# Two attentions rearranged as a pipeline of 128-row tiles

## Chip, core and metric
One core of a Trainium2 chip. The metric is the device time of the whole program in microseconds (us): three runs of the kernel before took 1804.64, 1805.28 and 1810.08 us.

## What is computed
One inference step of a two-layer decoder for 256 prompt tokens and 32 sample tokens (8 sequences of 4 new tokens, each with 256 past positions), all in fp32.

- Layer 0: RMSNorm, q/k/v projection, norm and rotary of each head, attention A with 16 heads of 64, output projection, dense SwiGLU. With 256 positions the block-sparse attention of the reference is a plain causal one. The past keys and values of a sample lie in two pages of 128 positions that a page table names.
- Shared keys and values for layer 1 from the stream behind layer 0.
- Layer 1: q projection for 3 groups x 8 heads, attention B: each head slot attends in three dilated windows and merges the three by their softmax denominators. That is one softmax over the three masked score sets together, with common keys and values. Output projection, then a top-2-of-8 mixture of SwiGLU experts, which takes more than half of the time.

The core of both attentions, from the reference:
```
sc = einsum('qhd,khd->qhk', q, k) * ATTN_SCALE       # masked
p = softmax(sc, axis=-1)                             # B: over its three groups
o = einsum('qhk,khd->qhd', p, v)
```

## The kernel before
Each matmul against weights is three matmuls of fp32r parts (whi, wlo; lines 241 to 243); attention matmuls are plain fp32, and each of those shows as two records. The work is written out by hand in one instruction stream per engine, with semaphores between them: SyncE issues the weight pieces into a ring of six, GpSimd issues the pages of the caches and the stores of new keys and values, TensorE multiplies and transposes, VectorE takes maxima and scales, ScalarE takes exponentials and copies.

Attention (`attend` on TensorE, ScalarE and VectorE) is a loop over ten steps t. Step t handles the prompt scores of head pair t (A) or head t (B), the keys of sample sequence t, the sample scores of t-1, the prompt values of t-1 and the sample values of t-2.

- Prompt scores (`scores`, line 524): per head and group two matmuls, queries 0 to 127 against keys 0 to 127 and queries 128 to 255 against all 256. In A the two heads of a pair lie in the two row halves of the array.
- `masked_max` (line 1202) adds the mask in PSUM and takes the row maximum; `exp` (line 933) writes probabilities with their sums; `probabilities` (lines 1212 to 1218) adds the groups and divides; `turn_probs` (line 567) transposes three blocks; ScalarE copies them (line 916); `values` (line 583) multiplies.
- Keys of a sequence: two page transfers (A: 512 KB each, `paged`, line 361; B: one transfer of both, `window`, line 378). `turn_keys` (line 558) transposes four 128x128 blocks at a time; ScalarE and in A VectorE copy them (lines 909, 1190).
- Sample scores of one sequence (line 541): for each pair of heads one matmul with a block-diagonal query block (`query_block`) of 64 columns in A and 96 in B, 288 key columns, all added up in one bank.
- Sample values of one sequence: transposes (line 593), then 16 matmuls in A and 8 in B with 128x128 value weights and 8 columns of probabilities (line 602). The new tokens' values of all sequences are one matmul for each pair at the very end (line 631).
- Output is split into high and low parts (lines 972 and 1296), then the output projection starts.

GpSimd's order (`caches`): keys of q, then values of q-1; keys wait for TensorE's transposes of the sequence that held the buffer, values for sample values three sequences back. The stores of new keys and values (lines 342, 343) stand behind the keys of sequence 0.

## Time and profile before

| | |
|---|---|
| median of three runs | 1805.28 us |
| profiled execution | 1809.19 us |
| its span | 1807.5 us |
| TensorE busy | 1710.8 us (95%) |
| VectorE busy | 1365.8 us (76%) |
| ScalarE busy | 1038.7 us (57%) |
| GpSimd busy | 56.0 us (3%) |
| mean granted TensorE clock | 0.958 |

The rows come from one execution, taken by the hardware profiler. PE is TensorE's matmuls, PEld its weight loads (beside them), DVE VectorE, ACT ScalarE, POOL GpSimd, SP SyncE. L12 is line 12 of the kernel. A granted clock of 1.00 is 2.4 GHz, 0.50 is 1.2 GHz. The page cuts the span in 40 slices of 45.2 us; attention A lies in slices 3 to 6, attention B in slices 14 to 16, the experts from slice 18 on. Ends of matmuls are modelled, and the busy time of matmuls that overlap is counted once. "<-" behind an idle time names what ended it. A chain of waits is followed back from the last instruction and shows what each stretch of time hung on.

### The profile page before, as it was taken

The page shows a single profiled execution, that of the slowest core. Times are in us where ns is not written, and L with a number is a line of the kernel's source. Part 1 is how long each engine was busy: PE and PEld are TensorE (multiplying, and loading weights), DVE is VectorE, ACT ScalarE, POOL GpSimd, SP SyncE. Part 2 cuts the span into 40 slices and gives each one's busy share as a digit, 9 for nine tenths or more (in the row PEclk, how much of TensorE's full clock was granted, in tenths as well). Part 3 has the DMA queues.
Part 4 walks back from the last instruction along what each step waited for, and adds up shares of the span by engine and source line. Part 5 has one row for each costly group of instructions (what it writes and reads, how often), then busy time and mean ns, then how long its engine had stood idle before and what let it go on. Part 6 is the DMA issues. An engine that isn't in the chain of part 4 may idle for free.

```text
span 1807.5 us, 24840 instructions
## 1 busy us (share of the span) xinstructions
PE 1710.8 (95%) x9068; PEld 1431.7 (79%) x9068; DVE 1365.8 (76%) x1732; ACT 1038.7 (57%) x1043; POOL 56.0 (3%) x81
## 2 busy tenths in 40 slices
PE   7998989999989798589999999999999999999998
PEld 6876779999987677467887888888878878878886
DVE  5864426565567685688898898898898888888987
ACT  5433324433444242457777777777777767777775
POOL 0001101000000110100000000000000000000000
PEclk9999869999999887699999999999999999999999
DMA  9346413543653421169999999999999999999995
GB/s 326 111 155 189 141 37 126 165 149 114 191 171 117 154 98 44 47 233 330 354 350 331 364 340 343 352 347 331 364 335 344 353 338 351 347 337 354 351 334 205
DMA packets 232982, 452.97 MB, mean 251 GB/s; under 512 B 7585, under 2 KB 79265, under 8 KB 232785
## 3 DMA queue, kind: packets, MB, share of 16 engines
q1 hardware_dynamic: 224656, 421.93, 66.8%
q0 software_dynamic: 8256, 30.12, 5.1%
q8 instruction: 43, 0.70, 0.2%
q14 instruction: 27, 0.21, 0.0%
HBM read 447.30 MB, written 4.72 MB: 250 GB/s over the span
## 4 chain that ended last, share of the span: by engine, by line
PE 86%; DVE 8%; ACT 3%; issue 2%; DMA 1%; POOLq 0%; DVEq 0%; SPq 0%; ACTq 0%; POOL 0%
PE psum L241 24%; PE psum L243 23%; PE psum L242 23%; PE psum L602 2%; PE psum L541 2%; PE psum L740 1%; PE psum L775 1%; PE psum L558 1%; PE psum L755 1%; DVE wlo L237 1%; ACT whi L233 1%; DVE rs L1152 1%; PE psum L583 1%; PE psum L479 1%; PE psum L488 1%
## 5 line engine op out<-in xcount | busy, mean ns | idle before, releaser
L237 DVE TENSOR_TENSOR wlo<-raw,whi 128x2048 fp32r<-128x2048 f32 (+1 forms) x404 | 911.7, 2262 | 208.1 <-ACT whi L233 207.7
L233 ACT ACTIVATE whi<-raw 128x2048 fp32r<-128x2048 f32 (+1 forms) x404 | 764.9, 1896 | 304.4 <-PE psum L243 304.3
L241 PE MATMUL psum<-whi,xgh 128*128 128x512 f32 x896 | 359.7, 401 | 8.5 <-DVE wlo L237 7.1
L243 PE MATMUL psum<-whi,xgl 128*128 128x512 f32 x896 | 355.7, 397 | 0.0
L242 PE MATMUL psum<-wlo,xgh 128*128 128x512 f32 x896 | 354.5, 396 | 0.0
L241 PE MATMUL psum<-hh,whi 128*128 128x288 f32 x800 | 248.4, 310 | 13.7 <-DVE hl L1296 9.1
L243 PE MATMUL psum<-hh,wlo 128*128 128x288 f32 x800 | 241.8, 302 | 0.0
L242 PE MATMUL psum<-hl,whi 128*128 128x288 f32 x800 | 241.1, 301 | 0.0
L241 PEld LDWEIGHTS psum<-whi,xgh 128*128 128x128 f32 x896 | 169.1, 189 | 50.6 <-DVE wlo L237 10.6
L243 PEld LDWEIGHTS psum<-whi,xgl 128*128 128x128 f32 x896 | 168.8, 188 | 41.1
L242 PEld LDWEIGHTS psum<-wlo,xgh 128*128 128x128 f32 x896 | 169.2, 189 | 39.1
L241 PE MATMUL psum<-whi,acth 128*128 128x512 f32 x448 | 178.3, 398 | 0.0
L242 PE MATMUL psum<-wlo,acth 128*128 128x512 f32 x448 | 178.2, 398 | 0.0
L243 PE MATMUL psum<-whi,actl 128*128 128x512 f32 x448 | 175.9, 393 | 0.0
L241 PEld LDWEIGHTS psum<-hh,whi 128*128 128x128 f32 x800 | 155.0, 194 | 22.1 <-DVE hl L1296 9.5
L242 PEld LDWEIGHTS psum<-hl,whi 128*128 128x128 f32 x800 | 155.3, 194 | 1.3
L243 PEld LDWEIGHTS psum<-hh,wlo 128*128 128x128 f32 x800 | 154.5, 193 | 0.0
L241 PEld LDWEIGHTS psum<-whi,acth 128*128 128x128 f32 x448 | 84.1, 188 | 20.7
L243 PEld LDWEIGHTS psum<-whi,actl 128*128 128x128 f32 x448 | 84.1, 188 | 20.5
L242 PEld LDWEIGHTS psum<-wlo,acth 128*128 128x128 f32 x448 | 84.2, 188 | 18.7
L1063 ACT ACTIVATE sg<-psum 128x512 f32<-128x512 f32 x56 | 33.5, 598 | 47.8 <-PE psum L243 47.7
L241 PE MATMUL psum<-gh,whi 128*128 128x288 f32 x176 | 52.1, 296 | 1.2 <-issue 1.2
(297 smaller groups left out, 1751.8 us busy)
## 6 DMA issues: line engine op xcount, KB each, us to landing
raw<-in_w_gu_moe SPq DMA_DIRECT2D x226, 1024.0 KB, 5.2
raw<-in_w_down_moe SPq DMA_DIRECT2D x112, 1024.0 KB, 5.3
raw<-in_w_gu_dense SPq DMA_DIRECT2D x22, 1024.0 KB, 5.1
raw<-in_w_qkv_a SPq DMA_DIRECT2D x12, 1024.0 KB, 12.8
raw<-in_w_down_dense SPq DMA_DIRECT2D x16, 704.0 KB, 4.6
kraw_a<-in_cache_a_k POOLq DMA_DIRECT2D x16, 512.0 KB, 4.6
vraw_a<-in_cache_a_v POOLq DMA_DIRECT2D x16, 512.0 KB, 4.8
raw<-in_w_q_b SPq DMA_DIRECT2D x6, 1024.0 KB, 5.0
```

The lines of the kernel that those rows point to most:

```text
L233: nc.scalar.activation(whi[:, p % SPL, 0:size], raw[:, p % RAW, 0:size], ACT.Copy).then_inc(hi_ready, 1)
L237: nc.vector.tensor_tensor(wlo[:, p % SPL, 0:size], raw[:, p % RAW, 0:size], whi[:, p % SPL, 0:size].bitcast(F32), ALU.subtract).then_inc(p ...
L241: nc.tensor.matmul(out, lh, rh, start=start, stop=False)
L242: nc.tensor.matmul(out, lh, rl, start=False, stop=False)
L243: return nc.tensor.matmul(out, ll, rh, start=False, stop=stop)
L479: nc.tensor.matmul(ps[6][:, 0:T], con("rot"), sq[:, 5 + r % 2], start=True, stop=True)\
L488: nc.tensor.matmul(bank[:, 0:T], cst[c:c + 32, slice(*CONST["headspread"])], rs[c:c + 32, 1], start=True, stop=True)\
L541: ins = nc.tensor.matmul(ps[SS_BANK][0:rows, 0:T], b["qblk"][:, u % 2, j * rows:(j + 1) * rows], b["keys"][:, j, :], start=j == 0, stop=j ...
L558: ins = nc.tensor.transpose(bank[:, i * P:(i + 1) * P], b["kraw"][:, u % b["nk"], pg, j * P:(j + 1) * P], con("ident"))
L583: ins = nc.tensor.matmul(out, b["vtok"][:, half, h * DH:(h + 1) * DH], b["pt"][:, h % 2, cols_], start=half == 0, stop=half == 1)
L602: ins = nc.tensor.matmul(out, b["vraw"][:, u % 2, c, j * P:(j + 1) * P], b["spt"][:, u % 2, c, 8 * j:8 * j + 8], start=c == 0, stop=c == 1)
L1063: nc.scalar.activation(sg[:, :], ps[0][:, :], ACT.Silu).then_inc(sem("silu_done"), 1)
```

## The change
Both attentions become a loop over jobs (`JOBS_A`, `JOBS_B`). A job is one 128-row tile of softmax: a prompt head ("p"), or a sample tile ("s"). A sample tile holds four pairs of heads x four sequences x two heads x four queries = 128 rows: four tiles in A, two in B.

In step t TensorE does the scores of job t, transposes the probabilities of job t-2 and multiplies the prompt values of job t-2; sample values of a tile come in steps t-3 and t-4 counted the same way. `FILLS` says how many key pages (now 128 positions x 512 columns, 256 KB) are transposed in each step: in A two in each of 16 steps, in B 4, 4, 0, 3, 3, 2.

Sample scores of a tile: for each group and each of four sequences four matmuls with 32 query columns, one to each 32-column group of the array, 288 key columns. Sample values: probabilities are the 32-column weights and the values stream, 128 columns at a time; the new tokens' values are one matmul of 512 columns for each column group. ScalarE scales the result by the denominators (`scale_out`), and `pick_rows` brings it back to head layout with eight matmuls.

The key buffer has six places in A and four in B, the value buffer four and three. A has three score banks in rotation; B has one set of three. GpSimd issues single key pages, and values of half a width in A, in an order given by `VALUES_A` and `VALUES_B`: the list holds for each value transfer the number of the key page behind which it is issued. In B the query block lies where the tokens of the new keys lay, so it waits for their stores. The masks of the samples grow in B; a constant of 32 columns goes.

```diff
+P_, S_ = "p", "s"
+JOBS_A = [(P_, 0), (P_, 1), (P_, 2), (P_, 3), (S_, 0), (P_, 4), (P_, 5), (P_, 6), (S_, 1), (P_, 7), (P_, 8), (P_, 9), (S_, 2),
+          (P_, 10), (P_, 11), (P_, 12), (S_, 3), (P_, 13), (P_, 14), (P_, 15)]
+JOBS_B = [(P_, 0), (P_, 1), (S_, 0), (P_, 2), (P_, 3), (P_, 4), (S_, 1), (P_, 5), (P_, 6), (P_, 7)]
+FILLS_A = [2] * 16
+FILLS_B = [4, 4, 0, 3, 3, 2]
+VALUES_A = [9] * 4 + [16, 16, 18, 18] + [24, 24, 26, 26] + [32] * 4
+VALUES_B = [7] * 3 + [16] * 5
...
+        A["score_banks"], A["pt_bank"], A["pv_bank"], A["kt_banks"], A["s_bank"] = ((0,), (1,), (7,)), 2, 3, (4, 5), 6
...
+        B["score_banks"], B["pt_bank"], B["pv_bank"], B["kt_banks"], B["s_bank"] = ((0, 1, 2),), 3, 4, (5, 7), 6
...
+            def key_page(b, n):
+                tg, slot = b["tag"], n % b["kring"]
+                z, q, page = n // 8, 4 * (n // (2 * b["nj"])) + n // 2 % 4, n % 2
+                if n >= b["kring"]:
+                    eng.wait_ge(sem(f"ktr_done_{tg}"), n - b["kring"] + 1)
+                if b is A:
+                    pg = eng.value_load(pgt[0:1, 2 * q + page:2 * q + page + 1], min_val=0, max_val=NPHYS - 1)
+                    src = io["cache_a_k"][0][bass.ds(pg, 1), :, 512 * (z % 2):512 * (z % 2) + 512].rearrange("a p n -> p (a n)")
+                else:
+                    src = io["cache_b_k"][q][P * page:P * page + P, :]
+                eng.dma_start(b["kraw"][:, slot, :], src).then_inc(sem(f"kraw_loaded_{tg}{slot}"), 16)
...
+            def value_pages(b, n):
+                tg, slot = b["tag"], n % b["vring"]
+                z, q = n // 4, 4 * (n // b["nj"]) + n % 4
+                if n >= b["vring"]:
+                    eng.wait_ge(sem(f"spv_done_{tg}"), n - b["vring"] + 1)
+                if b is A:
+                    for j in range(2):
+                        pg = eng.value_load(pgt[0:1, 2 * q + j:2 * q + j + 1], min_val=0, max_val=NPHYS - 1)
+                        eng.dma_start(b["vraw"][:, slot, j, :], io["cache_a_v"][0][bass.ds(pg, 1), :, 512 * (z % 2):512 * (z % 2) + 512]
+                                      .rearrange("a p n -> p (a n)")).then_inc(sem(f"vraw_loaded_{tg}{slot}"), 16)
+                else:
+                    eng.dma_start(b["vraw"][:, slot], io["cache_b_v"][q].rearrange("(j p) n -> p j n", p=P)).then_inc(sem(f"vraw_loaded_{tg}{slot}"), 32)
...
+            def caches(b, first):
+                v = 0
+                for n in range(first, 4 * b["nj"]):
+                    key_page(b, n)
+                    if n == first + 3:
+                        eng.wait_ge(sem(f"kv_stored_{b['tag']}"), 64)
+                    while v < 2 * b["nj"] and b["vafter"][v] == n:
+                        value_pages(b, v)
+                        v += 1
+                while v < 2 * b["nj"]:
+                    value_pages(b, v)
+                    v += 1
+            for n in range(A["kring"]):
+                key_page(A, n)
...
+            caches(A, A["kring"])
...
+                def banks_free(k):
+                    if k >= len(b["score_banks"]):
+                        eng.wait_ge(sem(f"exped_{tg}"), exped_count(b, k - len(b["score_banks"])))
...
+                def scores(k, h):
+                    banks_free(k)
+                    r, j = 64 * (h % 2), h // 2
+                    for g in range(ng):
+                        bank = ps[job_banks(b, k)[g]]
+                        q = b["qT"][r:r + 64, g * nj + j, :]
+                        nc.tensor.matmul(bank[:, 0:P], q[:, 0:P], b["kT"][r:r + 64, j, 0:P], start=True, stop=True)
+                        nc.tensor.matmul(bank[:, P:384], q[:, P:2 * P], b["kT"][r:r + 64, j, 0:2 * P], start=True, stop=True)                            .then_inc(sem(f"scored_{tg}"), 1)
...
+                def sample_scores(k, z):
+                    banks_free(k)
+                    eng.wait_ge(sem(f"keys_copied0_{tg}"), 4 * (z + 1))
+                    eng.wait_ge(sem(f"keys_copied1_{tg}"), 4 * (z + 1))
+                    eng.wait_ge(sem(f"new_keys_{tg}"), z + 1)
+                    eng.wait_ge(sem(f"qblk_{tg}"), z // (nj // 4) + 1)
+                    for g in range(ng):
+                        for s in range(4):
+                            for c in range(4):
+                                at_ = (4 * g + s) * b["qrow"] + 32 * (4 * z % nj + c)
+                                ins = nc.tensor.matmul(ps[job_banks(b, k)[g]][32 * c:32 * c + 32, 0:T], b["qblk"][:, at_:at_ + 32],
+                                                       b["keys"][:, s, c, :], start=s == 0, stop=s == 3)
+                        ins.then_inc(sem(f"scored_{tg}"), 1)
+                def turn_keys(n):
+                    slot = n % b["kring"]
+                    eng.wait_ge(sem(f"kraw_loaded_{tg}{slot}"), 16 * (n // b["kring"] + 1))
+                    if n >= 2:
+                        eng.wait_ge(sem(f"keys_copied{n % 2}_{tg}"), n // 2)
+                    for c in range(4):
+                        ins = nc.tensor.transpose(ps[b["kt_banks"][n % 2]][:, c * P:(c + 1) * P], b["kraw"][:, slot, c * P:(c + 1) * P], con("ident"))
...
+                def turn_probs(k, kind):
+                    eng.wait_ge(sem(f"probs_{tg}"), k + 1)
+                    if k >= 1:
+                        eng.wait_ge(sem(f"pt_copied_{tg}"), k)
+                    bank, p = ps[b["pt_bank"]], b["p"][:, k % b["ps"], 0]
+                    for c in range(2):
+                        nc.tensor.transpose(bank[:, c * P:(c + 1) * P], p[:, c * P:(c + 1) * P], con("ident"))
+                    w = P if kind == P_ else NSAMP
+                    nc.tensor.transpose(bank[0:w, 2 * P:3 * P], p[:, 2 * P:2 * P + w], con("ident")).then_inc(sem(f"pt_turned_{tg}"), 1)
...
+                def values(k, h):
+                    eng.wait_ge(sem(f"pt_copied_{tg}"), k + 1)
+                    if h % 2 == 0 and h >= 2:
+                        eng.wait_ge(sem(f"o_copied_{tg}"), h // 2)
+                    out, v = ps[b["pv_bank"]][64 * (h % 2):64 * (h % 2) + 64], b["vtok"][:, :, h * DH:(h + 1) * DH]
+                    nc.tensor.matmul(out[:, 0:2 * P], v[:, 0], b["pt"][:, h % 2, 0:2 * P], start=True, stop=False)
+                    nc.tensor.matmul(out[:, P:2 * P], v[:, 1], b["pt"][:, h % 2, 2 * P:3 * P], start=False, stop=True)                        .then_inc(sem(f"pv_done_{tg}"), 1)
...
+                def sample_values(k, z, part):
+                    j0 = 4 * z % nj
+                    if part == 0:
+                        eng.wait_ge(sem(f"pt_copied_{tg}"), k + 1)
+                        if z >= 1:
+                            eng.wait_ge(sem(f"so_copied_{tg}"), z)
+                        for c in range(4):
+                            new = b["vtok"][0:NSAMP, 2, (j0 + c) * P:(j0 + c + 1) * P].unsqueeze(1).to_broadcast([NSAMP, 4, P])
+                            nc.tensor.matmul(out_bank[32 * c:32 * c + 32, :].rearrange("p (s n) -> p s n", s=4),
+                                             b["spt"][0:NSAMP, 2 * P + 32 * c:2 * P + 32 * c + 32], new, start=True, stop=False)
+                    for s in (0, 1) if part == 0 else (2, 3):
+                        n = 4 * z + s
+                        slot = n % b["vring"]
+                        eng.wait_ge(sem(f"vraw_loaded_{tg}{slot}"), 32 * (n // b["vring"] + 1))
+                        for half in range(2):
+                            for c in range(4):
+                                ins = nc.tensor.matmul(out_bank[32 * c:32 * c + 32, s * P:(s + 1) * P],
+                                                       b["spt"][:, half * P + 32 * c:half * P + 32 * c + 32],
+                                                       b["vraw"][:, slot, half, c * P:(c + 1) * P], start=False, stop=s == 3 and half == 1)
+                        ins.then_inc(sem(f"spv_done_{tg}"), 1)
...
+                def pick_rows(z):
+                    eng.wait_ge(sem(f"so_scaled_{tg}"), z + 1)
+                    for s in range(4):
+                        for r in range(2):
+                            ins = nc.tensor.matmul(out_bank[64 * r:64 * r + 64, 16 * s:16 * s + 16], b["pvs"][:, s * P + 64 * r:s * P + 64 * r + 64],
+                                                   pick[:, s, r], start=True, stop=True)
+                    ins.then_inc(sem(f"picked_{tg}"), 1)
...
+                for t in range(len(b["jobs"]) + 3):
+                    kind, u = job_at(b, t)
+                    fills = fills_at(b, t)
+                    if kind == P_:
+                        scores(t, u)
+                    elif kind == S_:
+                        sample_scores(t, u)
+                    for n in fills[0:1]:
+                        turn_keys(n)
+                    kind2, u2 = job_at(b, t - 2)
+                    if kind2:
+                        turn_probs(t - 2, kind2)
+                    kind3, z = job_at(b, t - 3)
+                    if kind3 == S_:
+                        sample_values(t - 3, z, 0)
+                    kind4, z = job_at(b, t - 4)
+                    if kind4 == S_:
+                        sample_values(t - 4, z, 1)
+                    for n in fills[1:]:
+                        turn_keys(n)
+                    kind5, z = job_at(b, t - 5)
+                    if kind5 == S_:
+                        pick_rows(z)
+                    if kind2 == P_:
+                        values(t - 2, u2)
...
+                def scale_out(z):
+                    eng.wait_ge(sem(f"spv_done_{tg}"), 4 * (z + 1))
+                    nc.scalar.activation(b["pvs"][:, :], ps[b["s_bank"]][:, :], ACT.Copy, scale=b["sst"][:, z % 2, 8:9])                        .then_inc(sem(f"so_scaled_{tg}"), 1)
...
+                for t in range(len(b["jobs"]) + 3):
+                    fills = [n for n in fills_at(b, t) if n % 2 == 0]
+                    for n in fills[0:1]:
+                        copy_keys(n)
+                    kind2, u2 = job_at(b, t - 2)
+                    if kind2:
+                        copy_probs(t - 2, kind2, u2)
+                    kind5, z = job_at(b, t - 5)
+                    if kind5 == S_:
+                        scale_out(z)
+                    for n in fills[1:]:
+                        copy_keys(n)
+                    kind, u = job_at(b, t)
+                    if kind:
+                        exp(t, kind, u)
+                    kind3, h = job_at(b, t - 2)
+                    if kind3 == P_ and h % 2 == 1:
+                        eng.wait_ge(sem(f"pv_done_{tg}"), h + 1)
+                        nc.scalar.activation(b["oT"][:, h // 2, 0:SEQ], ps[b["pv_bank"]][:, 0:SEQ], ACT.Copy).then_inc(sem(f"o_copied_{tg}"), 1)
...
+                def new_keys(z):
+                    if z >= 1:
+                        eng.wait_ge(sem(f"scored_{tg}"), scored_count(b, b["jobs"].index((S_, z - 1))))
+                    for i in range(4):
+                        ins = V.tensor_copy(b["keys"][:, i, :, PAST:T], b["kT"][:, 4 * z % nj:4 * z % nj + 4, SEQ:T])
+                    ins.then_inc(sem(f"new_keys_{tg}"), 1)
...
+                def query_block(gr):
+                    if gr == 0:
+                        if ng > 1:
+                            eng.wait_ge(sem(f"kv_stored_{tg}"), 64)
+                        chain(V.memset(b["qblk"][:, :], 0.0))
+                    else:
+                        eng.wait_ge(sem(f"scored_{tg}"), scored_count(b, b["jobs"].index((S_, groups - 1))))
...
+                for t in range(len(b["jobs"]) + 3):
+                    kind, u = job_at(b, t)
+                    if t == (0 if ng == 1 else 1):
+                        query_block(0)
+                        new_keys(0)
+                    kind1, u1 = job_at(b, t - 1)
+                    if kind == P_:
+                        masked_max(t, u)
+                    elif kind == S_:
+                        sample_max(t, u)
+                    for n in fills_at(b, t):
+                        if n % 2 == 1:
+                            copy_keys(n)
+                    if kind1 == P_:
+                        probabilities(t - 1, u1)
+                    elif kind1 == S_:
+                        sample_probs(t - 1, u1)
+                        if u1 + 1 < 2 * groups:
+                            new_keys(u1 + 1)
+                        if u1 == groups - 1:
+                            query_block(1)
+                    kind5, z = job_at(b, t - 5)
```

## Rows read from the trace of the kernel before

**Rows 1.** The page's row of the granted clock in tenths, 40 slices.
```profile
PEclk9999869999999887699999999999999999999999
```

**Rows 2.** Chain of waits, attention A: start us, us, what ran.
```profile
127.66 1.03 DVE qblk_a L1169
...
160.42 0.80 PE psum L583 x8
...
165.09 0.86 PE psum L524 x8
165.95 1.02 PE psum L558 x8
...
167.78 0.48 PE psum L567 x3
...
169.46 3.55 PE psum L602 x32
...
265.87 0.61 PE psum L241
```

**Rows 3.** Grouped lines of attention A: count, busy us, mean ns, idle before.
```profile
L541 PE MATMUL psum<-keys_a,qblk_a 128*64 128x288 f32 x128 | 40.4, 479 | 1.0 <-DVE keys_a L1190 1.0
L602 PE MATMUL psum<-spt_a,vraw_a 128*128 128x8 f32 x256 | 34.2, 274 | 0.5 <-ACT sptn_a L952 0.5
...
L1190 DVE COPY keys_a<-psum 128x512 f32<-128x512 f32 x16 | 11.1, 691 | 9.0 <-PE psum L558 9.0
```

**Rows 4.** Windows in attention A: length, busy of PE, PEld, DVE, ACT, POOL, PEclk, DMA, GB/s.
```profile
136.00:140.00 4.00, 2.20 (x14) 1.04 (x12) 2.17 (x11) 0.59 (x2) 1.59 (x3) 1.00 0.92 248
140.00:144.00 4.00, 2.60 (x15) 2.60 (x16) 1.09 (x3) 1.08 (x2) 0.00 (x0) 0.75 0.78 288
190.00:195.00 5.00, 5.00 (x16) 2.29 (x14) 0.00 (x0) 0.00 (x0) 0.48 (x1) 0.68 0.65 213
```

**Rows 5.** Timeline of GpSimd: start us, us, engine, line, what, idle before.
```profile
134.29 0.55 POOL L361 DMA_DIRECT2D kraw_a<-in_cache_a_k  x1 [3.74 <-issue]
136.39 0.53 POOL L361 DMA_DIRECT2D kraw_a<-in_cache_a_k  x1 [1.54 <-issue]
...
147.52 0.53 POOL L361 DMA_DIRECT2D kraw_a<-in_cache_a_k  x1 [0.61 <-issue]
149.01 0.53 POOL L361 DMA_DIRECT2D vraw_a<-in_cache_a_v  x1 [0.97 <-issue]
150.15 0.53 POOL L361 DMA_DIRECT2D vraw_a<-in_cache_a_v  x1 [0.61 <-issue]
...
618.14 0.52 POOL L343 DMA_DIRECT2D out_bv<-vtok_b  x1
```

**Rows 6.** Timeline of TensorE in the q/k/v projection.
```profile
56.08 0.69 PE L471 MATMUL psum<-sq,cst 128*32 128x288 f32 x8
56.70 0.75 PE L479 MATMUL psum<-sq,cst 128*128 128x288 f32 x2
```

**Rows 7.** Chain of waits, attention B.
```profile
615.43 4.72 DMA kraw_b<-in_cache_b_k
...
648.34 2.16 PE psum L524 x12
...
663.40 0.79 PE psum L583 x4
...
713.03 0.61 PE psum L241
```

**Rows 8.** Timeline of all engines in one step of attention B.
```profile
644.22 0.17 DVE L1212 RECIPROCAL st_b<-st_b 128x2 f32<-128x2 f32 x1
...
645.80 0.35 DVE L1218 TENSOR_SCALAR p_b<-p_b,st_b 128x256 f32<-128x256 f32 x1
...
650.53 0.30 DVE L1202 CUSTOM_DVE_ANT_0 psum<-psum,mask_b 128x128 f32<-128x128 f32 x1 [0.26 <-PE psum L524]
...
654.41 0.21 ACT L933 ACTIVATION_READ_ACCUMULATOR p_b<-psum,st_b 128x1 f32 x1
```

More of the change, by code:

```diff
@@ new lines, in job_banks, with job_at, exped_count, scored_count @@
+        def job_banks(b, k):
+            return b["score_banks"][k % len(b["score_banks"])]
+        def job_at(b, k):
+            return b["jobs"][k] if 0 <= k < len(b["jobs"]) else ("", 0)
+        def exped_count(b, k):
+            return sum(2 if kind == P_ else 1 for kind, _ in b["jobs"][:k + 1])
+        def scored_count(b, k):
+            return b["ng"] * (k + 1)
+        def fills_at(b, t):
+            n = sum(b["fills"][:t])
+            return range(n, n + b["fills"][t]) if t < len(b["fills"]) else range(0)
@@ L696, in _ @@
             to_tokens(B)
[L697 removed]
+            attend(B)
             residual(P_WOB, tiles_wob, B["nj"], "wob", "o_split_b", hh, hl)
@@ L1611, in prompt, with sample @@
         return np.concatenate([m[0:P, 0:P], m[P:, :]], axis=1)
[L1613 to L1620 removed]
+    def sample(ok, gr):
+        pos = PAST + (i % QLEN)[:, None]
+        new = np.arange(NSAMP)[None, :]
+        own = new // QLEN == 4 * gr + (i[:, None] // 8) % 4
+        return ok(pos, np.arange(PAST)[None, :]), own & ok(pos, PAST + new % QLEN)
     causal = lambda q, k: k <= q
```

457 lines of the change are left out of this document (121 added, 336 removed).

## The prediction

> **What bounds the kernel now.** I read the page first: TensorE is busy 95% of the span, but its granted clock dips in slices 5 and 6 and in slices 14 to 17 of 45.2 us each, and those are the two attentions and what follows them [rows 1]. The expert stage behind them is dense and at full clock, and the change does not touch it, so only the length of the two attention stages can move. Then the chain of waits for attention A. It runs from 127.6 us (first scores) to 265.9 us (first matmul of the output projection), 138.3 us, and from 155 us on it is almost only TensorE: per sequence the sample scores, the prompt scores, page transposes, probability transposes, sample values and prompt values, one behind the other [rows 2]. The grouped lines say which are dear: sample scores (L541) 40.4 us, sample values (L602) 34.2 us [rows 3]. Both are wasteful. L541 streams 288 columns for 64 useful output columns; L602 loads 128x128 weights to stream 8 columns (32 records in 3.55 us, 0.11 us each). The stage windows show a second loss: between 190 and 195 us the clock is 0.68 with TensorE always busy, just behind such an L602 burst, and it falls to 0.75 after 136 to 140 us, where TensorE waited for pages [rows 4]. Attention B runs from about 615.0 to 713.0 us, 98 us [rows 7], and its timeline shows VectorE and ScalarE on the path too: maxima and exponentials of one tile take 4.09 us (650.53 to 654.62) [rows 8].
>
> **The change, attention A.** The new stage has 20 jobs (16 prompt heads, 4 sample tiles of 128 rows). TensorE's work, at full clock:
> - Prompt scores: two matmuls a head, 384 columns. Twelve records for three such pairs take 2.16 us [rows 7], so 0.72 us; 16 x 0.72 = 11.5 us. (Before, two heads in two row halves took 0.86 us [rows 2]; that overlap is lost, 4.6 us dearer in all.)
> - Prompt values: one head alone took 0.79 us [rows 7], two heads in two column halves 0.80 us [rows 2], so this overlap is lost too: 16 x 0.8 = 12.8 us.
> - Probability transposes: 20 x 0.48 = 9.6 us; key pages: 32 times four transposes, eight take 1.02 us, so 16.3 us [rows 2].
> - Sample scores: 64 matmuls as before, but each fills a 32-column group and four neighbours go to four groups. The trace has exactly this form: the head sums, four 128x32 matmuls (8 records) over 288 columns of different data; the next matmul starts 0.62 us later, while one 128x128 matmul of the same width shows 0.75 us [rows 6]. So four go in the time of one: 16 waves x 0.62 = 9.9 us against 40.4.
> - Sample values: per tile 32 matmuls over 128 columns in 8 waves, and four over 512 columns with 32 rows. No row has this. From below: 128/288 of 0.62 = 0.28 us a wave; from above: 8 records alone at L602's 0.11, 0.88 us. I take 0.35, nearer to the form of rows 6; the wide wave is 512/288 x 0.62 = 1.1 us. A tile 3.9 us, four 15.6 (between 13 and 33).
> - Picking rows: eight small matmuls a tile; from 0.6 us (half of L602's rate) to 1.8 us. I take 1.2, in all 4.8.
>
> Sum 80.5 us. Waits come on top. Prompt values stand one page behind the transposes whose ScalarE copy they need; after fills end nothing is between. I take 0.5 us (0 to 0.9) for each of 20 jobs, 10 us. VectorE's work on a tile of A is at most half of that on a tile of B (maxima 2.1 and probabilities 1.9 us [rows 8], one group in place of three), 20 x 2 us, plus 16 page copies at 0.69 us [rows 3], some 51 us; ScalarE has a similar share: neither binds. The chain of one tile spans three steps and is hidden.
>
> What can hurt is GpSimd's queue. It issues, in order, 26 key pages (six stand loaded) and 32 value halves of 256 KB, where it issued 30 transfers of 512 KB; each needs a page number read first. Neighbouring issues are 1.14 us apart (149.01, 150.15), 1.49 when the kind changes (147.52, 149.01), once 2.10 (134.29, 136.39) [rows 5]. I take 1.3: 58 x 1.3 = 75 us, from about 131 us to 206. It is as long as TensorE's own 80, and the two wait for each other: behind key page 9 stand eight value issues, 10 us with no key page, while TensorE needs two pages a job. Value pages wait for sample values of earlier tiles, and keys queue behind them. Landing adds 4.7 us [rows 7]. I charge 6 us for this coupling and, since TensorE stands for some us in that burst, 3 us of half clock. Last, splitting the output stays (265.9 minus the end of the last copy, 4.8 us). End: 127.6 + 80.5 + 10 + 6 + 3 + 4.8 = 231.9, say 230 since the last values overlap. Against 265.9: 36 us saved (10 to 53).
>
> The Trainium skill (DMA: Bandwidth & Descriptors, Anatomy of one DMA) gives about 2 us plus the bytes at 436 GB/s, an estimate of 2.6 us for 256 KB; the trace shows 4.7 us for 512 KB, longer than the 3.2 of that rule. By it pages would land 2 us earlier and the sum would stay, since issue and not landing sets the pace here.
>
> The skill (TensorEngine Tiling (Array Packing), Key Properties) says that a change of tiling mode drains the array, which speaks against more, smaller jobs. By the trace such changes lie inside the durations I use (0.86 to 1.02 us pieces that follow one another directly [rows 2]); some 25 further changes at 0.1 us would be an estimate of 2.5 us.
>
> **Attention B.** Here one set of three score banks serves all jobs, so a job's scores wait for the exponentials of the one before. A prompt step: scores 2.16 us, with the maxima of the first two groups beside them; of the 4.09 us for maxima (2.1) and exponentials two thirds of the maxima (1.4) are hidden; 2.16 + 2.7 + 0.1 = 4.9 us. VectorE must fit the probabilities of the tile before (644.22 to 646.15, 1.9 us [rows 8]) and page copies into that gap of 2.7 us: I add 0.5, 5.4 us (4.9 to 6.5). A sample step: 12 waves x 0.62 = 7.4, then 2.3 for last maximum and a wider exponential: 9.7. Everything else of TensorE hides in the gaps. The start is slow: pages 4 to 7 stand behind the four store issues, which end at 618.7 now with one page issue before them [rows 5] and near 620.2 with four shorter ones; the pages land at 625 to 626; the query block is now written where the keys of the stores lie, so VectorE waits for those stores to land (about 625) with the maxima of job 1 queued behind, then writes block and new keys (4 us), maxima and page copies (3.5 us): the first sample job starts near 632.5. Then 2 x 9.7 + 6 x 5.4 = 51.8, to 684.3; the last tile's probabilities, transposes, copy, values, copy and splitting 7.1 us: 691.4. Half clock in the waits of the start 1.5: 693 against 713.0, 20 us saved (5 to 31).
>
> **The start.** Six key pages (1.5 MB) are fetched where 1 MB was, in the weight-bound first 45 us: the 0.5 MB more cost up to 1.4 us; I take 1. The constants lose 32 columns and the B mask grows, both away from any wait: nothing.
>
> **Sum.** 1 - 36 - 20 = -55 us. The profiled execution of before took 1809.2 us (span 1807.5, 1.7 around it), so its counterpart would be 1754; the median of the runs is 1805.3, and from it 1750 us.
>
> **Rivals.**
> - No waits: tiles flow and GpSimd keeps ahead at 1.14 us (66 us, done at 197). For it: TensorE and the queue need the same time. Against: in-order coupling. A ends at 127.6 + 80.5 + 4.8 = 213 (-53), B at its lower bound (-29): 1805 + 1 - 82 = 1724.
> - GpSimd's queue paces A at 2.1 us an issue, as once in rows 5: 58 x 2.1 = 122 us, last issue at 253, then landing, last sample tile and splitting, 271: A +5, B -20, start +1: 1791. Against: the other intervals are 1.14 and 1.49.
> - Column groups do not run together: 64 sample-score matmuls at 0.5 us, 32 us (+22), values 41 us (+25), A at 277 (+11); in B 96 score matmuls 48 us against 15 on the chain (+33), 713 + 13: 1805 + 25 = 1830. It decides from about half of the overlap lost. Against: rows 6, whose records overlap.
> - Half clock through both stages: a TensorE that works in pieces between waits is granted 1.2 GHz. Each us of TensorE's work costs one more: A +80 less what the queue hides (15), B +27: 55 saved against 92 lost, 1842; slower from some 60% of the work at half clock. For it: after the wait of 136 to 140 us the clock fell to 0.75 [rows 4]. Against: the same window shows 1.00 at 55% busy; only a longer stand or an L602 burst was followed by a fall, and those bursts vanish. The Trainium skill (TensorE: Matmul & The Clock Gate, Part 1) has the clock set by how busy TensorE was shortly before; the rows agree as far as they go.
>
> **How the numbers follow.** Forecast 0.63, no waits 0.18, slow queue 0.10 (0.02 of it no change), groups serial 0.05, half clock 0.04 (0.01 of it no change). Predicted 1750. Range: from the no-waits case, 1722, to the slow queue, 1790; it takes in A 10 to 53 and B 5 to 31 but not all ends at once. A change within 0.3% (5 us) can't be told from none here. Faster 0.89, same 0.03, slower 0.08.
>
> **What would show it.** Attention A's projection starts near 230 us, B's stage is about 78 us long. The sample-score line costs 10 us in A and 15 in B; sample values 16 us in A. GpSimd issues A's pages 1.1 to 1.5 us apart almost without idling between 135 and 206 us, and TensorE's largest wait in A is for key pages. In B scores wait for ScalarE's exponentials each job. The expert stage keeps its length. I am wrong if head groups show up one after another, if the clock row stays at 5 through either stage, or if the saving sits in another stage.

## The result and the profile after

The changed kernel takes 1783.03 us (median of 4 runs, 1781.34 to 1783.73) against 1807.68 for the kernel before on the same chip (4 runs): ratio 0.9865, 95% interval 0.985 to 0.988. It is 25 us faster, where 55 were forecast. All other ratios below are also against the kernel before, measured beside the experiment.

First the page: span 1782.0 us (before 1807.5), and its clock row, to be laid beside [rows 1].

```profile
span 1782.0 us, 25119 instructions
PEclk9997789999999777699999999999999999999999
kraw_a<-in_cache_a_k POOLq DMA_DIRECT2D x32, 256.0 KB, 3.3
```

The dips are still there: 7 and 7 in slices 4 and 5 (134 to 223 us), and slices 14 to 17. The third line says that a key page of 256 KB lands 3.3 us after its issue.

I measure each stage from its first prompt scores to the first matmul of the output projection, and count how many us of it ran at 1.2 GHz (a granted clock of 0.5) and not at 2.4. The windows' mean clock agrees: A's 0.77 is 1 less half of 54.4 in 120.3. (The expectations below carry these counts about 2 us too high, 56.5 for A and 52 for B.) From one profiled execution of each:

| | before | after | forecast |
|---|---|---|---|
| A, length | 138.2 (127.6 to 265.9) | 120.3 (127.8 to 248.1) | 102.4 |
| A, at 1.2 GHz | 48.8 | 54.4 | a cost of 3 |
| A, TensorE waits for key pages | 4.0 | 16.3 | a cost of 6 |
| B, length | 98.0 (615.0 to 713.0) | 93.4 (594.1 to 687.5) | 78 |
| B, at 1.2 GHz | 31.7 | 50.1 | a cost of 1.5 |
| between A and B | 349.1 | 346.0 | 349 |
| after B | 1094.5 | 1094.5 | same |

So 17.9 us came from A, 4.6 from B, 3.1 from the stretch between (5.6 us less of it at 1.2 GHz). The start, for which 1 us more was forecast, took 0.2 more. The windows of both stages, A and B of the kernel before, then A and B of the changed one, columns as in [rows 4]:

```profile
127.62:265.87 138.25, 123.53 (x753) 93.98 (x753) 51.38 (x198) 45.00 (x139) 18.59 (x34) 0.82 0.41 132
614.98:713.03 98.05, 85.58 (x464) 65.33 (x464) 70.26 (x373) 34.15 (x94) 14.06 (x20) 0.84 0.29 98
```
```profile
127.80:248.08 120.28, 94.96 (x797) 61.44 (x797) 45.24 (x183) 44.04 (x123) 33.72 (x62) 0.77 0.47 147
594.10:687.55 93.45, 75.17 (x590) 49.27 (x590) 49.81 (x196) 28.10 (x62) 16.93 (x28) 0.73 0.31 104
```

TensorE is busy 95 of 120 us in A, and the mean granted clock of the stage is 0.77. The grouped lines of A answer to [rows 3] (columns: count, busy us, mean ns, idle before):

```profile
L593 PE MATMUL psum<-cst,kraw_a 128*128 128x128 f32 x128 | 26.2, 342 | 16.7 <-DMA kraw_a<-in_cache_a_k 16.3 <-DVE keys_a L1234 0.4
L634 PE MATMUL psum<-vraw_a,spt_a 128*32 128x128 f32 x256 | 9.6, 296 | 0.0
L582 PE MATMUL psum<-keys_a,qblk_a 128*32 128x288 f32 x128 | 8.6, 408 | 0.4
L646 PE MATMUL psum<-cst,pvs_a 128*64 128x16 f32 x64 | 3.4, 241 | 2.3 <-ACT pvs_a L981 2.3
```

The sample scores (L582) went from 40.4 to 8.6 us and the sample values (L634, with 5.1 us at L626) from 34.2 to 14.7, to which the picks (L646) add 3.4: the part of the change that looked most daring worked. What grew is in the first line: 16.3 us in which TensorE stood for a key page. GpSimd's timeline (columns as in [rows 5]) shows where they come from:

```profile
155.52 0.54 POOL L395 DMA_DIRECT2D kraw_a<-in_cache_a_k  x1 [0.62 <-issue]
163.07 0.54 POOL L407 DMA_DIRECT2D vraw_a<-in_cache_a_v  x1 [7.02 <-PE psum L634]
...
173.72 0.54 POOL L407 DMA_DIRECT2D vraw_a<-in_cache_a_v  x1 [0.60 <-issue]
174.87 0.54 POOL L395 DMA_DIRECT2D kraw_a<-in_cache_a_k  x1 [0.61 <-issue]
...
190.90 0.54 POOL L407 DMA_DIRECT2D vraw_a<-in_cache_a_v  x1 [9.75 <-PE psum L634]
...
218.44 0.54 POOL L407 DMA_DIRECT2D vraw_a<-in_cache_a_v  x1 [10.62 <-PE psum L634]
```

GpSimd mostly issues 1.14 to 1.16 us apart, and stands three times, 7.0, 9.8 and 10.6 us, for the sample values that free a place for a value page. Behind the first two of these stands wait key pages whose places have long been free (that of page 17 since 154.5 us, that of page 25 since 179.4); behind the third wait value pages alone. So TensorE's 16.3 us have three sources: 10.2 us for key pages 17, 19, 25 and 27, behind the first two stands; 3.7 us for page 10, behind eight value issues (139.5 to 147.4 us) that wait for nothing; and 2.4 us for page 6, which lands 7.4 us after its issue, beside the four stores. Pages are counted from 0. The chain of waits shows the other end of the queue, and what the clock does next:

```profile
130.30 7.98 DMA out_av<-vtok_a
...
148.58 3.30 DMA kraw_a<-in_cache_a_k
...
156.93 0.59 PE psum L593 x4
...
163.80 2.15 PE psum L582 x32
...
174.87 3.35 DMA kraw_a<-in_cache_a_k
178.26 1.12 PE psum L593 x4
...
202.65 3.30 DMA kraw_a<-in_cache_a_k
205.99 1.12 PE psum L593 x4
...
248.08 0.61 PE psum L279
```

Key page 19, for instance, is issued at 174.87, lands at 178.2, and TensorE waits for it. Behind it the same four transposes take 1.12 us instead of 0.59: TensorE has stood, and the granted clock is at 0.5 from 169.8 to 186.9. It is so again from 200.5 to 214.2, behind the stand that ends at 199.0 and through that before 206.0, and from 149.3 to 156.1, which begins in the stand for page 10.

B, from its chain of waits, to be laid beside [rows 7]:

```profile
595.61 4.71 DMA kraw_b<-in_cache_b_k
...
614.28 6.03 PE psum L582 x96
...
639.24 1.04 PE psum L593 x4
640.92 1.86 PE psum L626 x8
642.78 1.86 PE psum L634 x32
644.64 1.05 PE psum L593 x4
645.69 1.05 PE psum L614 x2
647.16 6.20 PE psum L582 x96
...
653.84 1.01 PE psum L634 x32
...
675.87 4.04 DMA vraw_b<-in_cache_b_v
...
687.55 0.61 PE psum L279
```

96 sample scores take 6.03 us (7.4 forecast). But the prompt step from 636.2 to 647.2 takes 11.0 us where 5.4 were forecast. Nearly all of it is TensorE's work, and from 637.4 on, at 1.2 GHz, its pieces have twice their length: the same 32 sample values take 1.86 us at 642.78 and 1.01 at 653.84.

### The profile page after: what moved, and what is told of

Its sections match the earlier page's. It is cut to its first block, busy times and chain, and to the rows that moved or that the text cites. A ratio compares the mean times of both kernels' runs of the same rounds, so it can differ in the third digit from the quotient of the medians.

```text
span 1782.0 us, 25119 instructions
## 1 busy us (share of the span) xinstructions
PE 1669.5 (94%) x9238; PEld 1382.0 (78%) x9238; DVE 1339.1 (75%) x1540; ACT 1032.0 (58%) x995; POOL 76.3 (4%) x121
## 4 chain that ended last, share of the span: by engine, by line
PE 85%; DVE 6%; ACT 3%; issue 2%; DMA 2%; POOLq 0%; POOL 0%; DVEq 0%; SPq 0%; ACTq 0%
PE psum L279 24%; PE psum L281 23%; PE psum L280 23%; PE psum L783 1%; PE psum L818 1%; PE psum L593 1%; DVE wlo L275 1%; PE psum L798 1%; PE psum L569 1%; PE psum L582 1%; ACT whi L271 1%; DVE rs L1187 1%; PE psum L568 1%; PE psum L523 1%; PE psum L634 1%
## 5 line engine op out<-in xcount | busy, mean ns | idle before, releaser
L279 PEld LDWEIGHTS psum<-whi,xgh 128*128 128x128 f32 x896 | 169.4, 189 | 50.9 <-DVE wlo L275 10.6
L279 PEld LDWEIGHTS psum<-hh,whi 128*128 128x128 f32 x800 | 153.5, 192 | 21.3 <-DVE hl L1320 9.0
L1098 ACT ACTIVATE sg<-psum 128x512 f32<-128x512 f32 x56 | 33.6, 600 | 47.8 <-PE psum L281 47.7
```

The costliest lines, as they stand in the source:

```text
L279: nc.tensor.matmul(out, lh, rh, start=start, stop=False)
L1098: nc.scalar.activation(sg[:, :], ps[0][:, :], ACT.Silu).then_inc(sem("silu_done"), 1)
```

## The experiments

**Is it the order of issues in A?** The only edit is behind which key page each value page is issued.

```
-VALUES_A = [9] * 4 + [16, 16, 18, 18] + [24, 24, 26, 26] + [32] * 4
+VALUES_A = [10, 11, 12, 13] + [19, 19, 21, 21] + [27, 27, 29, 29] + [32] * 4
```

> Against the changed kernel (1783.0 us median, attention A 120.3 us from first scores to projection, 56.5 us of it at half clock, 16.3 us of TensorE waiting for key pages). Only the order of GpSimd's transfers in A is changed: first four values spread behind key pages 10 to 13, the next ones behind 19 and 21, 27 and 29. Theory O (three times key pages stand behind value issues that wait for sample values; TensorE stands, and half clock follows): the waits for key pages fall from 16 us to under 5, half clock in A to under 35 us, A takes 95 to 103 us, the kernel 1759 to 1767 us. Rival C (TensorE's other short gaps keep the clock low whatever the pages do): the page waits go, but half clock stays near 50 us, A takes 106 to 112 us, 1769 to 1775 us. Rival Q (GpSimd's issue rate of 1.14 us is the limit itself): under 4 us change, 1779 to 1784 us.

Measured: 1762.45 us, ratio 0.9757 (0.9738 to 0.9777), 20.6 us below the changed kernel. A's window:

```profile
127.70:233.91 106.21, 88.69 (x796) 55.85 (x797) 45.14 (x183) 43.47 (x123) 33.64 (x62) 0.84 0.53 167
```

A is 106.2 us, 33.6 at 1.2 GHz, page waits 6.7. The kernel's time and the clock are where theory O had them; A and the page waits are a little over its bounds, in a profiled execution that was the slowest of five (1769.9 us). The number of issues and their pace (1.15 us) did not change, so a queue that is slow in itself (rival "slow queue") is ruled out as what lengthened A.

A second order goes further, one value page at a time between keys:

```
+VALUES_A = [11, 12, 14, 15] + [19, 20, 21, 22] + [27, 28, 29, 30] + [32] * 4
```

> As the first reordering (which gave 1762.5 us and A of 106.2 us, still 6.7 us of waits for key pages), but with single value transfers spread between single key pages: behind 11, 12, 14, 15, then 19 to 22, then 27 to 30. Theory O: waits for key pages 2 to 5 us, A 100 to 105 us, the kernel 1756 to 1762 us. Rival: the 1.14 us an issue is the bound by now (58 issues, 66 us, and stores ahead): 1761 to 1765 us.

Measured: 1760.84 us, ratio 0.974 (0.972 to 0.9759). A is 99.1 us. Its window and its waits (waiter, waited for: us in total, times, longest):

```profile
127.80:226.92 99.12, 84.09 (x796) 53.98 (x796) 45.22 (x183) 43.66 (x123) 33.62 (x62) 0.88 0.57 179
```
```profile
POOL vraw_a L407 <- PE psum L634: 6.9, 3, 5.0
PE psum L593 <- DMA kraw_a<-in_cache_a_k: 4.1, 2, 2.5
```

And the same two of the changed kernel:

```profile
POOL vraw_a L407 <- PE psum L634: 28.6, 4, 10.6
PE psum L593 <- DMA kraw_a<-in_cache_a_k: 16.3, 6, 3.7
```

GpSimd's stands fall from 28.6 to 6.9 us, TensorE's from 16.3 to 4.1 (2.5 of it for page 6, as before), its busy time from 95.0 to 84.1 with the same work: 21 us of A by order alone. By the kernel's time the two orders can't be told apart (0.974 and 0.9757, intervals overlapping).

**What all of A's supply costs.** The 26 key pages past the first six are not fetched in A; the tiles are computed from what the ring holds. The value pages are fetched and waited for as before.

```
+                if b is A and n >= b["kring"]:
+                    return
...
-                    eng.wait_ge(sem(f"kraw_loaded_{tg}{slot}"), 16 * (n // b["kring"] + 1))
+                    eng.wait_ge(sem(f"kraw_loaded_{tg}{slot}"), 16 if b is A else 16 * (n // b["kring"] + 1))
```

> Attention A without the 26 later key pages: they are not fetched, the transposes read the six pages loaded at the start again (this part of the computation is left out); values are fetched as before, with the same waits. It is the lower end of what page supply can cost. Theory O: TensorE never stands for keys, A takes 92 to 100 us, the kernel 1755 to 1763 us, half clock under 30 us. Rival C: A 104 to 112 us, half clock over 45 us, 1767 to 1775 us. If values are what TensorE waits for, A stays above 112 us.

Measured: 1753.31 us, ratio 0.9717 (0.9693 to 0.9741). A's window:

```profile
127.60:218.56 90.96, 79.66 (x797) 50.92 (x797) 45.13 (x183) 43.50 (x123) 19.70 (x36) 0.92 0.37 120
```

A is 91.0 us, a little under theory O's 92 to 100, so 29.3 of its 120.3 us hang on key pages. TensorE's busy time falls from 95.0 to 79.7 us for the same number of matmuls, which is 15.3 of the 29.3; the other 14.0 are idle time (the 16.3 of page stands are gone, waits elsewhere grew by 2.3). For the 15.3 the clock is the candidate (54.4 us at 1.2 GHz in the changed kernel, 13.7 here), which the next run tests. The order of e7 brings back 21 of the 29.

**The clock's part alone.** The order of the transfers stays; 128 idle transposes of constants stand in front of five waits for key pages.

```
-                    eng.wait_ge(sem(f"kraw_loaded_{tg}{slot}"), 16 * (n // b["kring"] + 1))
...
+                    if b is A:
+                        for _ in range({10: 20, 17: 30, 19: 24, 25: 30, 27: 24}.get(n, 0)):
+                            nc.tensor.transpose(ps[b["kt_banks"][n % 2]][:, 0:P], con("featsum"), con("ident"))
+                    eng.wait_ge(sem(f"kraw_loaded_{tg}{slot}"), 16 * (n // b["kring"] + 1))
```

> The changed kernel, GpSimd's order as it is, with 128 idle 128x128 transposes on TensorE in A: 20 to 30 just ahead of each of its waits for key pages 10, 17, 19, 25 and 27 (0.11 us each at full clock). Theory O with clock: the stand for pages stays as idle or filled time (16 us), but TensorE is not slow behind it: half clock in A falls from 56 us to 25 to 40, A from 120 to 108 to 115 us, the kernel 1771 to 1778. Rival (half clock in A costs nothing, since the pages set the time): A 119 to 124 us, 1782 to 1787.

Measured: 1774.63 us (1768.78 to 1780.48), ratio 0.9824 (0.9801 to 0.9847). A's window:

```profile
126.50:234.54 108.04, 91.50 (x924) 63.98 (x924) 44.86 (x183) 43.67 (x123) 33.61 (x62) 0.96 0.52 164
```

A is 108.0 us, with 8.1 at 1.2 GHz: 12.3 us shorter with GpSimd's order unchanged, so the clock had a cost of its own. This profiled execution was the fastest of the four; by the medians the kernel is 8.4 us faster. The transposes themselves take some 14 us (127 of them recorded, at 0.11 us), of which the waits hide only a part, so the clock's cost in A is larger than what this run gives back. The Trainium skill (TensorE: Matmul & The Clock Gate, Part 1) has the clock follow how busy TensorE was shortly before. The trace agrees: transposes without any use raised A's mean granted clock from 0.77 to 0.96.

**Do the column groups run together?** The two inner loops of the sample scores change places, so that four neighbours go to one column group.

```
-                        for s in range(4):
-                            for c in range(4):
+                        for c in range(4):
+                            for s in range(4):
```

> The changed kernel with the two inner loops of the sample scores exchanged: the four sequences of one 32-column group follow one another, so neighbouring matmuls use the same group. Same number of matmuls and same sums. In the changed kernel 32 records take 2.15 us in A and 96 take 6.1 us in B. If column groups run together only when neighbours use different groups: the four tiles of A take 6.5 to 8 us each (+18 to +23 us in all), the two of B 19 to 24 us each (+26 to +36), the kernel 1815 to 1840 us (A may hide some behind pages). If the overlap does not depend on order (records pipelined anyway): within 3 us of 1783.

Measured: 1803.87 us, ratio 0.9978 (0.9968 to 0.9988). The chain of waits of this kernel, one tile of A and one of B:

```profile
161.36 5.10 PE psum L582 x32
...
616.88 13.13 PE psum L582 x96
```

The same 32 records take 5.10 us against 2.15, 96 take 13.1 against 6.03. B is 109.9 us (+16.5), A 124.4 (+4.1). So the groups do run together in the changed kernel, and nearly all of its gain over the kernel before (20.8 of 24.7 us) hangs on the order of two loops. The loss was smaller than I expected (tiles of 6.5 to 8 us in A, the kernel at 1815 or more): it is a factor of 2.2 to 2.4, not of 4. Four neighbours in one group also add up in the same place of PSUM; whether the group or that place holds them apart, no run tells.

**B: a late value page?** The ring gets a fourth place, in the places of two key pages that are no longer needed.

```
-            kraw=70656, ktok=78848, qblk=78848, spt=85120, mask=86656, kring=4, vring=3, ps=2, jobs=JOBS_B, fills=FILLS_B))
+            kraw=70656, ktok=78848, qblk=78848, spt=85120, mask=86656, kring=4, vring=4, ps=2, jobs=JOBS_B, fills=FILLS_B))
...
+                if b is B and n == 3:
+                    eng.wait_ge(sem(f"ktr_done_{tg}"), 14)
```

> In attention B the value buffer gets a fourth place, over the key places of pages 12 and 13 once these are transposed, so that all four sequences of a sample tile are loaded before the first is used; before, the last value page was issued at 675.9 us, when a place came free, and TensorE stood 4.0 us for it. Theory: B is 93.6 us long, becomes 87 to 91, the kernel 1777 to 1780 us. Rival: the sample part is beside the last tile's own chain (exponentials, probabilities, transposes, copy) and nothing is saved, 1782 to 1784 us.

Measured: 1782.27 us, ratio 0.9871 (0.9843 to 0.9899): no difference from the changed kernel. TensorE no longer waits for a value page, B is 95.2 us, 55.5 at 1.2 GHz, where 87 to 91 were expected: the rival holds. The chain's piece "675.87 4.04 DMA" is the transfer's own time; TensorE's own stand for value pages in B was 0.8 us, and taking it away gained nothing.

**B: the clock?** 60 idle transposes in the places where TensorE stands for VectorE and ScalarE.

```
+                WARM = {} if b is A else {0: 16, 1: 8, 3: 4, 4: 4, 5: 4, 8: 8, 9: 8, 10: 8}
...
+                    if t and t in WARM:
+                        if t >= 3:
+                            eng.wait_ge(sem(f"pt_copied_{tg}"), t - 2)
+                        warm(WARM[t])
...
+                    if t == 0:
+                        warm(WARM.get(0, 0))
```

> Attention B with idle transposes of 128x128 on TensorE where it waits anyway: 16 behind the first scores, 8 ahead of the scores of jobs 1, 8, 9 and 10, four ahead of those of jobs 3, 4 and 5; in all 60, 13 us of work at full clock. They wait for nothing and give nothing. Theory W (the low clock in B comes from the gaps that TensorE waits in, and it is what makes B's steps long): half clock in B falls from 52 us to under 35, B takes 84 to 90 us against 93.6, the kernel 1773 to 1780 us. Rival (B hangs on VectorE's and ScalarE's chain, clock is beside): B 94 to 100 us since the added work is partly in the way, 1783 to 1790 us.

Measured: 1778.89 us, ratio 0.9844 (0.9821 to 0.9868). B's window:

```profile
597.50:686.04 88.54, 72.74 (x651) 48.61 (x651) 48.66 (x196) 28.29 (x62) 16.87 (x28) 0.87 0.33 109
```

B is 88.5 us with 22.3 at 1.2 GHz (50.1 in the changed kernel). The 13 us that I gave for the transposes were wrong: 60 at 0.11 us are 6.6. The clock rose, but the gain in time is not settled by this run. The two intervals against the kernel before overlap, and B's length, 4.9 us shorter here, was anything from 90.8 to 93.7 us in five profiled executions with unchanged code in B (the changed kernel, e1, e4, e6, e7).

**B: supply and clock together.** First the 12 later key pages and the 5 later value pages of B are not fetched; then the same with 86 idle transposes (the expectation says 90).

```
+                if b is B and n >= b["kring"]:
+                    return
...
+                if b is B and n >= b["vring"]:
+                    return
...
-                    eng.wait_ge(sem(f"kraw_loaded_{tg}{slot}"), 16 * (n // b["kring"] + 1))
+                    eng.wait_ge(sem(f"kraw_loaded_{tg}{slot}"), 16 if b is B else 16 * (n // b["kring"] + 1))
...
-                        eng.wait_ge(sem(f"vraw_loaded_{tg}{slot}"), 32 * (n // b["vring"] + 1))
+                        eng.wait_ge(sem(f"vraw_loaded_{tg}{slot}"), 32 if b is B else 32 * (n // b["vring"] + 1))
```
```
+                WARM = {} if b is A else {0: 16, 1: 12, 3: 6, 4: 8, 5: 8, 6: 4, 8: 8, 9: 10, 10: 8, 11: 6}
```

> Attention B without the supply of pages: the 12 later key pages and the 5 later value pages of B are not fetched (the tiles are computed from what the ring holds). The forecast had B at 78 us, the changed kernel takes 93.4. Theory (half clock and TensorE's own pieces at that clock): only the stand for a value page near 676 us goes (at most 3 us), B is 88 to 93 us, with 45 us or more at 1.2 GHz. Rival (B waits for its supply as A did): B falls by 8 us or more, to 85 or less, and the half clock falls with it below 30 us.

> The same kernel without the later pages of B, and 90 idle transposes (0.11 us each at full clock, 9.9 us) in the places where TensorE stands for VectorE and ScalarE in B. Theory (half clock is what lengthened B's steps): half clock falls below 20 us and B to 80 to 86 us; what is then left above 78 is the last two jobs, whose sample values, picks and copies follow one another. Rival (the steps are set by the exponentials' chain and by VectorE whatever the clock): B stays at 88 us or more with the clock up.

Measured: without pages 1783.33 us, ratio 0.9863 (0.9843 to 0.9882); with the transposes too 1772.03 us, ratio 0.9799 (0.9782 to 0.9816). B's windows, first without pages, then with transposes:

```profile
596.70:686.22 89.52, 71.09 (x590) 46.96 (x591) 49.60 (x196) 28.20 (x62) 6.82 (x11) 0.78 0.13 44
```
```profile
591.10:675.00 83.90, 72.54 (x676) 50.69 (x677) 48.75 (x196) 28.17 (x62) 6.79 (x11) 0.90 0.13 46
```

Without pages B is 89.5 us, within the theory's bounds of 88 to 93, with 39.1 at 1.2 GHz (45 or more were expected), and the run as a whole gained nothing. With the transposes, B is 83.9 us with 16.5 at 1.2 GHz. The times of the two runs do not overlap (1781.6 to 1785.0 and 1770.8 to 1772.8), so here the transposes' gain is clear of noise. The theory holds for B: its supply hardly matters, its clock does. Not all of the 11.3 us between the two medians need be B's (5.6 in the profiles); A, whose code is the same in both, was 120.9 and 117.4 us in the two profiled executions.

**Order and transposes together.** The order of e7, the transposes of e5 in B, and 20 more in A's last steps.

```
+VALUES_A = [11, 12, 14, 15] + [19, 20, 21, 22] + [27, 28, 29, 30] + [32] * 4
+                WARM = {17: 4, 18: 6, 19: 4, 20: 6} if b is A else {0: 16, 1: 8, 3: 4, 4: 4, 5: 4, 8: 8, 9: 8, 10: 8}
```

> The second reordering in A, idle transposes in B as in the run before (B fell from 93.4 to 88.5 us there), and 20 more in A behind the last pages (ahead of the scores of jobs 17 to 19 and in step 20). If both effects add: 1750 to 1758 us, A 98 to 104 us and B 87 to 90 us. If they don't: 1758 to 1764.

Measured: 1754.29 us (1749.24 to 1761.48), ratio 0.9691 (0.966 to 0.9722). That is 29 us below the changed kernel and inside the 1750 to 1758 expected if both effects add. In its profiled execution, the slowest of the four, A is 101.1 and B 92.4 us (21.0 and 35.8 at 1.2 GHz), no shorter than e7's 99.1 and 90.8, and B misses its 87 to 90. Its median is 6.5 us lower than e7's, but the intervals just overlap: how much the transposes add to the order is not settled.

## Why the prediction was wrong in size

The direction and the first reason were right; the forecast failed in one step of A and one of B, and in both the clock is the larger part. The stages split into TensorE's work as it would be at full clock, what 1.2 GHz adds to it, and TensorE's idle time. For the second I take half of the time in which TensorE was busy at 1.2 GHz (A 42.6 us before and 43.6 after, B 26.3 and 40.7), since its pieces take twice as long there: transposes follow one another at 0.21 us there and at 0.11 at full clock. The forecast's idle time in A is its 10 us of waits, 6 of coupling and 4.8 of splitting, less the 1.9 by which it rounded down. In us:

| | forecast | before | after |
|---|---|---|---|
| A, work at full clock | 80.5 | 102.3 | 73.2 |
| A, added by 1.2 GHz | 3 | 21.3 | 21.8 |
| A, TensorE idle | 18.9 | 14.7 | 25.3 |
| B, work at full clock | not given | 72.5 | 54.8 |
| B, added by 1.2 GHz | 1.5 | 13.1 | 20.4 |
| B, TensorE idle | not given | 12.5 | 18.3 |

**A, TensorE's work (80.5 us): right in kind, and 7 us too dear.** Sample scores 2.15 us a tile (2.48 forecast), sample values 1.01 for 32 records and 0.99 for the wide wave, 3.0 us a tile (3.9), picks 0.65 at full clock (1.2). Without the key pages, e4's stage is 91.0 us, and the forecast without its terms for coupling and clock was 127.6 to 221, 93.4. That the two are so near is in part luck: e4 has 74.5 us of work and 11.3 idle, less than forecast, and 5.1 us that 1.2 GHz adds.

**A, "I charge 6 us for this coupling" and "3 us of half clock": this step failed.** Together it is 29.3 us (e4), 14.0 of idle time and 15.3 of slower work, where 9 were charged. I had seen that value pages wait for sample values of earlier tiles and keys queue behind them, and then priced the queue by its mean: 58 issues at 1.3 us, 75 us beside 80 us of work. Its pace was even better (1.14 us). What counts is the order: the queue stood for 7 and 10 us in the first of four value pages, whose release lies some jobs on, with the keys of the next job behind it. I should have followed for each value page when the place that it needs comes free. GpSimd "almost without idling" was a sign that I had named, and it did not come: its stands for places are 28.6 us. The eight value issues behind key page 9 I had seen, 10 us with no key page; they cost TensorE 3.7 us: key page 10 is issued behind them at 148.58 and lands at 151.9.

**A, the clock.** I took the fall of the clock as a small addition to one burst: 3 us, where 1.2 GHz adds 21.8. It stays low for 3 to 17 us at a time (139.1 to 142.5, 149.3 to 156.1, 169.8 to 186.9, 200.5 to 214.2, 227.8 to 238.1, and from 244.9 past the end of the stage). The first four begin in a stand for a key page or up to 1.5 us behind one, the fifth follows no page stand, the last begins in the wait for the split output. So the page stands, 16.3 us, cost about as much again in slower work (15.3). The kernel before lost 21.3 us to the clock too, in a stage where TensorE was busy 89% of the time: five of its seven falls in A (172.7, 186.4, 203.4, 217.1 and 230.7 us) came with TensorE busy without a gap, in or right behind a burst of L602. The prediction was right that these bursts vanish; the stands took their place, and the forecast's 80.5 us, all at full clock, took the loss as gone.

**B, "Half clock in the waits of the start 1.5", and steps of 5.4: failed.** 1.2 GHz adds 20.4 us. B's parts, in us:

| | forecast | after | e10 (no pages, transposes) |
|---|---|---|---|
| stage start to first sample job | 17.5 | 20.2 | 18.9 |
| from there to the last job's scores | 46.4 | 53.3 | 49.5 |
| from there to the projection | 12.5 | 19.9 | 15.5 |
| sum | 76.4 | 93.4 | 83.9 |

Of the 17 us over the forecast 9.5 are gone in e10. Idle transposes stand on its chain of waits themselves:

```profile
620.00 0.80 PE psum L659 x6
...
639.71 0.59 PE psum L659 x4
...
653.67 1.02 PE psum L659 x8
...
665.02 1.02 PE psum L659 x8
...
668.18 0.81 PE psum L659 x6
```

Without these 4.2 us the stage would be below 80, near the 78 forecast; that subtraction is argued, not run. "Everything else of TensorE hides in the gaps" was true at full clock only: at 1.2 GHz the step with page turns, new values and sample values is 11.0 us and sets the pace itself; in e10 the same step (633.2 to 640.2) is 7.0. The end was also too short: behind the last job's scores come transposes, new values and sample values of two jobs, not one chain of 7 us. The wait of 4.7 us for B's first pages was in the forecast.

**Rivals.** Serial column groups: refuted, and e3 shows what serial sample scores would have cost (20.8 us). The rival's 80 were too many: it had 8 us for the 16 matmuls (32 records) of a tile of A where even one group at a time takes 5.1; its part for the sample values no run made serial. Slow queue: refuted by the pace of 1.14 us and by e1. Half clock throughout: as a whole refuted, but 104.5 us of the two stages' 214 did run at 1.2 GHz, so it named the right mechanism, and 0.04 was too small for it. No waits: not met by any run with all pages; e7's A of 99 us comes nearest to its 85. The changes of tiling mode: the prediction's 0.1 us each fits, since transposes at full clock follow one another at 0.109 us and the next matmul of another tiling starts 0.203 us behind the last of them.

**What stays open.** B's remaining 6 us over the forecast in e10, part of which is the idle transposes' own time; whether transposes in B gain anything while its pages are fetched (e5, e8); why page 6 lands so late; and whether another order of B's page turns would bring more. Stage A differed by 6 us between profiled executions of unchanged code (117.4 to 123.7), so stage differences below that are not read as findings.

## What to carry to other kernels

A queue of transfers issued in order isn't priced by issues times pace: walk it entry by entry, and ask of each wait in it what stands behind; put an issue where its place is already free. And price each stand of TensorE twice, once as time and once for the clock behind it, before planning other work into "gaps" at full-clock durations; where gaps can't be closed, transposes of constants in them are worth a run.

## What the runs showed of the hardware that was not expected

- Here four 128x32 matmuls ran together only where neighbours went to different column groups: 32 records (288 columns) 2.15 us so, 5.10 us with four neighbours in one group. The Trainium skill (TensorEngine Tiling (Array Packing), Key Properties) says that different tiles can load and multiply in parallel; the trace agrees for neighbours in different groups, and e3 adds that the order of issue decides.
- GpSimd's issue with a page number read before it: 1.14 us apart whether 256 KB pages of keys or of values; one lands in 3.3 us (median), 512 KB took 4.7.
- A transpose of constants costs 0.11 us at full clock, and with 128 of them in its waits a stage of 120 us had 8.1 us at 1.2 GHz instead of 54.4, and was 12.3 us shorter in that execution; the transposes themselves took some 14 us.
